# The routed-expert stage of a one-layer decoder kernel: expert block in another order, weight pieces of 1 MB, x gathered straight into its tile

## The reference

```python
e_flat = eidx.reshape(-1)                 # 1024 tokens x 8 experts
...
padded = (counts + EXPERT_BLOCK - 1) // EXPERT_BLOCK * EXPERT_BLOCK   # blocks of 128 rows, each of one expert
...
xb = x_pad[row_tok].reshape(n_blocks, EXPERT_BLOCK, d)

def expert_block(args):
    xblk, e = args
    hid = jax.nn.silu(xblk @ w_gate[e]) * (xblk @ w_up[e])
    return hid @ w_down[e]

yb = lax.map(expert_block, (xb, block_e)).reshape(n_rows, d)
y = jax.ops.segment_sum(yb * row_w[:, None], row_tok, num_segments=t + 1)
```

## Time and profile before

| | |
|---|---|
| median of 3 runs | 2982.41 us (2974.08 to 2987.12) |
| the profiled execution, its time | 2998.25 us |
| its span in the profile | 2996.7 us |
| PE busy over the span | 2573.5 us (86%) |
| expert stage, 1865 to 2850 us: PE busy | 901.49 of 985 us |
| the same stretch: DVE, ACT, POOL busy | 669.34, 602.02, 414.89 us |
| the same stretch: share of DMA time in use | 0.78 |

### The profile page before, as it was taken

The page is one execution under the profiler, slowest core; times in us unless marked ns, Lnnn a source line. Parts: engine busy times, 40 slices in busy tenths (PEclk is TensorE's granted clock), DMA queues, the critical chain, the costliest instruction groups (busy, mean ns, idle before and its releaser), DMA issues. The chain is left out here.

```text
span 2996.7 us, 39317 instructions
## 1 busy us (share of the span) xinstructions
PE 2573.5 (86%) x12548; PEld 2072.5 (69%) x12549; DVE 1864.5 (62%) x2441; ACT 1264.2 (42%) x1673; POOL 766.6 (26%) x888
## 2 busy tenths in 40 slices
PE   7989998998999999969977832899999989998956
PEld 5768777777877777747856721677777767776832
DVE  3346887787788655527446613676677676667428
ACT  3343453354345333335221102566566675566400
POOL 2012111222211111100002072444444444444300
PEclk9999999999999999989989965999999999999978
DMA  5423345342322353263543135788778787879367
GB/s 117 67 44 63 64 47 53 64 57 50 78 54 47 71 78 78 61 207 123 170 149 105 60 72 171 249 282 274 256 279 284 268 304 261 263 262 331 129 268 320
DMA packets 246349, 462.96 MB, mean 154 GB/s; under 512 B 26649, under 2 KB 151065, under 8 KB 244191
## 3 DMA queue, kind: packets, MB, share of 16 engines
q1 hardware_dynamic: 211870, 377.44, 45.1%
q0 software_dynamic: 34368, 84.04, 8.0%
HBM read 399.97 MB, written 93.87 MB: 165 GB/s over the span
## 5 line engine op out<-in xcount | busy, mean ns | idle before, releaser
L58 PE MATMUL dn_pj<-x_hi,dn_hi 128*128 128x512 f32 x1024 | 437.7, 427 | 5.1 <-DVE dn_lo L924 2.9
L60 PE MATMUL dn_pj<-x_hi,dn_lo 128*128 128x512 f32 x1024 | 411.0, 401 | 0.0
L59 PE MATMUL dn_pj<-x_lo,dn_hi 128*128 128x512 f32 x1024 | 409.8, 400 | 0.0
L1008 DVE SCALAR_TENSOR_TENSOR uc_half<-u_in,par,uc_half 128x512 f32<-128x512 f32 x480 | 383.3, 798 | 13.1
L2250 DVE TENSOR_TENSOR e_lo<-e_raw,e_hi 128x1024 fp32r<-128x1024 f32 x256 | 340.4, 1389 | 74.1 <-ACT e_hi L2193 68.0
L58 PE MATMUL gu_ps<-e_hi,xg_hi 128*128 128x512 f32 x744 | 317.8, 427 | 56.2 <-DVE xg_lo L2255 32.0
L2193 ACT ACTIVATE e_hi<-e_raw 128x1024 fp32r<-128x1024 f32 x256 | 251.9, 1052 | 141.6 <-DMA e_raw<-in_w_gate_e_dram 116.5
L60 PE MATMUL gu_ps<-e_hi,xg_lo 128*128 128x512 f32 x744 | 300.2, 403 | 0.0
L59 PE MATMUL gu_ps<-e_lo,xg_hi 128*128 128x512 f32 x744 | 300.0, 403 | 0.0
L1147 POOL TENSOR_TENSOR a_lvl<-a_t,lvl_mask 128x512 f32<-128x512 f32 x112 | 167.7, 1514 | 349.0 <-PE dn_a L686 221.1
L60 PEld LDWEIGHTS dn_pj<-x_hi,dn_lo 128*128 128x128 f32 x1024 | 198.5, 194 | 45.8
(11 more groups left out here) (346 smaller groups left out, 5183.1 us busy)
## 6 DMA issues: line engine op xcount, KB each, us to landing
e_raw<-in_w_gate_e_dram SPq DMA_DIRECT2D x128, 512.0 KB
e_raw<-in_w_up_e_dram SPq DMA_DIRECT2D x128, 512.0 KB
e_raw<-in_w_down_e_dram SPq DMA_DIRECT2D x128, 512.0 KB
dn_raw<-in_w_in_dram SPq DMA_DIRECT2D x64, 512.0 KB
y_rows<-y_rows SPq DMA_DIRECT2D x8, 2560.0 KB, 30.7
y_rows<-y_rows SPq DMA_DIRECT2D x8, 1536.0 KB, 25.1
gate_rows<-qkv_next SPq DMA_DIRECT2D x16, 512.0 KB, 3.1
br_raw<-in_w_oa_dram SPq DMA_DIRECT2D x16, 512.0 KB
```

What stands on the lines that cost most here:

```text
L58: nc.tensor.matmul(out, w_hi, x_hi, start=first, stop=False)
L59: nc.tensor.matmul(out, w_hi, x_lo, start=False, stop=False)
L60: return nc.tensor.matmul(out, w_lo, x_hi, start=False, stop=last)
L1008: ins = stt(out=uc[:], in0=u_in[:, t:t + HALF], scalar=w, in1=uc[:], op0=ALU.mult, op1=ALU.add)
```

## The change

The raw tiles become three of 1 MB, each filled by two DMAs of 512 KB: gate|up of k 0 to 3, gate|up of k 4 to 7, and down. ACT and DVE split each in one instruction. Gate|up is still split two experts ahead, down now one ahead, with semaphores of its own (`dhi_s`, `dlo_s`). On PE a block now is: wait for `hidden` of the block before, gate|up k 0 to 3, transposes of that `hidden`, transposes of the next x, the register loads for the next expert, gate|up k 4 to 7, down of the block before. ACT and DVE run the three splits between the other steps of a block. `x_landing` and POOL's copy are gone: the indirect DMA writes `x_gather` itself, and so is issued only when PE has transposed the block before. A second small DMA (`credit_d[1]`) sets `xg_in` off at 16.

```diff
-PIECES = 6
+GU = 2
 BUFS = 3
-SLOTS = 6
 LAG = 4
-raw = [sb(ctx, f"e_raw{q}", [P, 4 * FF]) for q in range(SLOTS)]
+raw = [sb(ctx, f"e_raw{i}", [P, 2, 4 * FF]) for i in range(GU + 1)]
...
-xl_d = sb(ctx, "x_landing", [P, D])
...
-    if i < 4:
-        ks, w = slice(4 * (i // 2), 4 * (i // 2) + 4), i % 2
-        return raw[i][:].rearrange("p (k f) -> p k f", k=4), wh[j][:, ks, w, :], wl[j][:, ks, w, :]
-    return raw[i][:], dh[j][:, i - 4, :], dl[j][:, i - 4, :]
+    if i < GU:
+        wkf = lambda w: w[j][:, 4 * i:4 * i + 4, :, :].rearrange("p k w f -> p w k f")
+        return raw[i][:].rearrange("p w (k f) -> p w k f", k=4), wkf(wh), wkf(wl)
+    return raw[i][:], dh[j][:], dl[j][:]
...
+    def load_gate_up(e, first):
+        for i in range(GU):
             if not first:
+                sp.wait_ge(lo_s, e * GU + (i + 1 - GU))
+            for n, w in enumerate((a["w_gate_e"], a["w_up_e"])):
+                src = w[0, bass.ds(e, 1)].rearrange("o (p k) f -> p (o k) f", k=KT)[:, 4 * i:4 * i + 4, :]
+                sp.dma_start(raw[i][:, n, :].rearrange("p (k f) -> p k f", k=4), src).then_inc(w_in[i], 16)
+    def load_down(e, first):
+        if not first:
+            sp.wait_ge(dlo_s, e)
+        for n in range(2):
+            src = a["w_down_e"][0, bass.ds(e, 1)].rearrange("o (c p) n -> p (o c) n", p=P)[:, n, :]
+            sp.dma_start(raw[GU][:, n, :], src).then_inc(w_in[GU], 16)
+    load_gate_up(0, True)
+    load_down(0, True)
+    load_gate_up(1, False)
+    with sp.Fori(2, E) as e:
+        load_gate_up(e, False)
+        load_down(e - 1, False)
+    load_down(E - 1, False)
...
-    def gather(n, column):
+    def rows(n, column):
         alone(pool, self.passed)
+        pool.wait_ge(xg_in, n * 16 + 16)
         g.tensor_copy(idx_g[:], self.tok_tab[:, column]).then_inc(idx_c, 1)
         g.tensor_copy(late_rows[:, bass.ds(n + LAG, 1)], self.row_tab[:, column]).then_inc(idx_l, 1)
         pool.wait_ge(idx_c, n + 1)
-        alone(pool, self.passed)
-        pool.indirect_dma_start(xl_d[:], None, self.x1_d, bass.IndirectOffsetOnAxis(idx_g[:, 0:1], 0),
-                                bounds_check=S - 1, oob_is_err=False).then_inc(xg_in, 16)
-    def hand_over(n):
-        pool.wait_ge(xg_in, n * 16 + 16)
+    def gather(n):
         pool.wait_ge(t_done, n * 2 + 2)
         alone(pool, self.passed)
-        g.tensor_copy(xg[:], xl_d[:]).then_inc(x_here, 1)
-        pool.wait_ge(x_here, n + 1)
+        pool.indirect_dma_start(xg[:], None, self.x1_d, bass.IndirectOffsetOnAxis(idx_g[:, 0:1], 0),
+                                bounds_check=S - 1, oob_is_err=False).then_inc(xg_in, 16)
     def scatter(n):
...
     with pool.Fori(0, E) as e:
-        nb, base = plan(pool, e)
+        nb, base = blocks(pool, e), first_block(pool, e)
         with pool.Fori(0, nb) as b:
             n = base + b
-            gather(n, bass.ds(e * NT + b, 1))
+            rows(n, bass.ds(e * NT + b, 1))
+            gather(n)
             scatter(n)
-            hand_over(n)
-    total = pool.value_load(self.plan[0:1, E - 1, 1:2], min_val=0, max_val=MAXB - 1) + \
-        pool.value_load(self.plan[0:1, E - 1, 0:1], min_val=1, max_val=NT)
+    total = first_block(pool, E - 1) + blocks(pool, E - 1)
     for late in range(LAG):
         scatter(total + late)
         if late == 0:
-            pool.wait_ge(t_done, total * 2 + 2)
-            pool.sem_inc(x_here, 1)
+            gather(total)
...
     def transposes(gb):
-        pe.wait_ge(x_here, gb + 1)
+        pe.wait_ge(xg_in, gb * 16 + 32)
         xv = xg[:].rearrange("p (c k) -> p k c", k=KT)
...
-    def down(j, gb):
+    def down(e, j, gb):
+        pe.wait_ge(dlo_s, e + 1)
         pe.wait_ge(hl_s, gb + 1)
...
-    def blk(e, j, j_prev, gb, first):
-        pe.wait_ge(xl_s, gb * 2 + 1)
-        if first:
-            pe.wait_ge(lo_s, e * PIECES + 2)
-        gate_up(j, range(0, 4))
-        pe.wait_ge(xl_s, gb * 2 + 2)
-        if first:
-            pe.wait_ge(lo_s, e * PIECES + 4)
-        gate_up(j, range(4, 6))
-        transposes(gb + 1)
-        gate_up(j, range(6, 8)).then_inc(gu_done, 1)
-        if j_prev is not None:
-            down(j_prev, gb - 1)
-        hid_t(gb)
...
+    def run(experts):
+        nb, base = blocks(pe, experts[0][0]), first_block(pe, experts[0][0])
+        for i, (e, j, _) in enumerate(experts):
+            following = experts[i + 1][0] if i + 1 < len(experts) else None
+            loaded = []
+            def blk(b, gb, first):
+                prev = not first or not isinstance(e, int) or e > 0
+                if prev:
+                    pe.wait_ge(hid_s, gb)
+                pe.wait_ge(xl_s, gb * 2 + 1)
+                if first:
+                    pe.wait_ge(lo_s, e * GU + 1)
+                gate_up(j, range(0, 4))
+                if prev:
+                    hid_t(gb - 1)
+                pe.wait_ge(xl_s, gb * 2 + 2)
+                transposes(gb + 1)
+                if first:
+                    if following is not None:
+                        loaded.extend((blocks(pe, following), first_block(pe, following)))
+                    pe.wait_ge(lo_s, e * GU + 2)
+                gate_up(j, range(4, 8)).then_inc(gu_done, 1)
+                if prev and first:
+                    down(e - 1, (j + BUFS - 1) % BUFS, gb - 1)
+                elif prev:
+                    down(e, j, gb - 1)
+            expert(pe, e, nb, base, blk)
+            if following is not None:
+                nb, base = loaded
     transposes(0)
-    all_experts(pe, expert)
-    nb, base = plan(pe, E - 1)
-    pe.wait_ge(lo_s, E * PIECES)
-    down((E - 1) % BUFS, base + nb - 1)
+    all_experts(pe, run)
+    nb, base = blocks(pe, E - 1), first_block(pe, E - 1)
+    pe.wait_ge(hid_s, base + nb)
+    hid_t(base + nb - 1)
+    down(E - 1, (E - 1) % BUFS, base + nb - 1)
...
-    def blk(gb, prev, split):
-        split(0, 1, 2, 3)
-        act.wait_ge(gu_done, gb + 1)
-        A(sg[:], gu[:, 0, :], ACT.Silu).then_inc(sg_s, 1)
-        for b in range(2):
-            act.wait_ge(t_done, gb * 2 + 5 + b)
-            x_hi(b)
-        if prev:
-            y_move(gb - 1)
-        act.wait_ge(ht_done, gb + 1)
-        A(hh[:], ht[:], ACT.Copy).then_inc(hh_s, 1)
-        split(4, 5)
...
+            def blk(b, gb, first):
+                def split(i):
+                    ahead = 2 if i < GU else 1
+                    if first and (not isinstance(e, int) or e + ahead < E):
+                        hi((j + ahead) % BUFS, nth + (j + ahead) // BUFS, i)
+                prev = not first or not isinstance(e, int) or e > 0
+                split(0)
+                if prev:
+                    hid_hi(gb - 1)
+                act.wait_ge(t_done, gb * 2 + 5)
+                x_hi(0)
+                split(1)
+                act.wait_ge(gu_done, gb + 1)
+                A(sg[:], gu[:, 0, :], ACT.Silu).then_inc(sg_s, 1)
+                act.wait_ge(t_done, gb * 2 + 6)
+                x_hi(1)
+                split(2)
+                if prev:
+                    y_move(gb - 1)
...
-    def blk(e, b, gb, split):
-        split(0, 1, 2, 3)
-        dve.wait_ge(sg_s, gb + 1)
-        v.scalar_tensor_tensor(out=hid[:], in0=sg[:], scalar=self.wt_tab[:, bass.ds(e * NT + b, 1)],
-                               in1=gu[:, 1, :], op0=ALU.mult, op1=ALU.mult).then_inc(hid_s, 1)
-        x_lo(gb + 1, 0)
-        x_lo(gb + 1, 1)
+    def hid_lo(gb):
         dve.wait_ge(hh_s, gb + 1)
         tt(hl[:], ht[:], hh[:].bitcast(F32), ALU.subtract).then_inc(hl_s, 1)
-        split(4, 5)
...
+                split(0)
+                if not first or not isinstance(e, int) or e > 0:
+                    hid_lo(gb - 1)
+                x_lo(gb + 1, 0)
+                dve.wait_ge(sg_s, gb + 1)
+                v.scalar_tensor_tensor(out=hid[:], in0=sg[:], scalar=self.wt_tab[:, bass.ds(e * NT + b, 1)],
+                                       in1=gu[:, 1, :], op0=ALU.mult, op1=ALU.mult).then_inc(hid_s, 1)
+                x_lo(gb + 1, 1)
+                split(1)
+                split(2)
```

127 lines of the change are left out of this document (58 added, 69 removed).

## The result

| | before | after |
|---|---|---|
| median | 2984.01 us (2974.08 to 2987.12, 4 runs) | 3110.49 us (3097.31 to 3114.42, 4 runs) |
| ratio, 95% interval | | 1.0422 [1.0381, 1.0463] |
| span of the profiled execution | 2996.7 us | 3112.9 us |

The account below looks back on a forecast made before the run. PE, busy 86% of the span, was taken as the bound, with the raw tile's loop longest in runs. Savings of 26 us outside runs and 20 in them, 46 from 2982.4, gave 2937 us; range 2887 to 2976.

Parts of the forecast that it names:

- The two regimes: Expert stage: later blocks bound by PE; runs of one-block experts with PE, DVE, ACT and DMA all heavily used.
- PE's floor: Expert stage: a block's 46 matmuls take PE at least 9.43 us at full clock.
- The waits for x's low part, for `hidden` and for registers: PE's waits of 32.0, 28.0 and 22.8 us: first mostly gone, second loses its place, about 15 of the third gone.
- Landing copy and sizes of the splits: DVE saves 0.68 us per first block without POOL's copy; doubled splits take at most 2.44 us on DVE, 2.10 on ACT.
- So it is hidden and costs nothing: The direct gather, issued about 4.1 us into a block, has 8.4 us to land and needs at most 7.1.
- The 4.7: Gather's landing time, 4.7 us from its issue to the start of its copy, in the profile before.
- is issued earlier relative to nothing: The scatter behind the gather must land before `y_block` is written, a wait of 32.2 us in 12 cases before.
- no change: Rival: y's late scatter holds ACT at `y_block`, 45 us go back in 64 first blocks, time 2982 us; chance 0.14.
- One of the prediction's own signs of being wrong: The forecast is wrong if ACT waits for the scatter in most blocks.
- slower: the raw tile's loop: Rival: a 1 MB tile refills only once wholly split; a 7.0 us load gives 13.2 us periods, 3010 us; chance 0.10.
- The landing of 4.9 us: Load of 1 MB into a raw tile, making the loop 11.1 us and saving 20 us in the runs.
- What was forecast for the new order: PE's waits for `hidden` and x's low part mostly go; the 57 periods outside runs fall to 9.6 us, saving 26.

Follow-up runs that it names:

- e8: The changed kernel with six pieces of 512 KB instead of the 1 MB pieces; 3020.4 us, ratio 1.0114 to the kernel before.
- e7: The kernel before with the new order alone, keeping 512 KB pieces and the landing copy; 3023.3 us, ratio 1.0135.
- e13: The changed kernel with POOL's steps reordered, scatter ahead of the wait for the landed gather and the next gather; 3033.1 us, ratio 1.0145.
- e10: The changed kernel with DVE's split of each 1 MB piece made in two halves; 3067.2 us, ratio 1.0274 to the kernel before.
- e12: The changed kernel with 512 KB pieces and POOL's steps reordered so the scatter precedes the gather's wait; 2964.3 us, ratio 0.9909.
- e18: e12 with ACT's `hid_hi` and DVE's `hid_lo` moved between the two 512 KB splits; 2960.6 us, ratio 0.9903 to the kernel before.

## Why the prediction was wrong

**What bounds the kernel.** The two regimes and PE's floor held: later blocks take 9.3 us wherever nothing stalls. The waits for x's low part, for `hidden` and for registers went about as counted (32.0 to 1.4, 28.0 to 12.0 in one wait, 22.8 to 7.9 us).

**Landing copy and sizes of the splits.** Right and small. DVE's split of 2048 took 2.29 us and ACT's 1.91, against bounds of 2.44 and 2.10. With direct gather a DVE split of 1024 takes 1.22 us in e8. But e7 and e8 differ by 3 us: without the copy and with the later gather the time is nearly the same.

**"So it is hidden and costs nothing": the gather.** It held for PE, which waited 11.2 us in the stage beyond the start, though the gather landed in 7.2 us, not 4.7. The 4.7 was the start of a copy, and 26 waits of the copy say when a gather was late, not how long it usually takes under another load.

**The scatter: the step that failed.** The forecast's own sum has no term for it: the scatter "is issued earlier relative to nothing" and stands at zero. It was counted only as a rival, "no change", with a sum of 4.1 + 1.0 + 1.1 + 4.7 = 10.9 against 9.4 for the end of down, 1.5 us late, of which 0.7 us would reach PE in each first block. All three terms were too small. From transposes to scatter it is 3.8 us, not 2.1: 0.9 us pass between the end of the transposes and the gather, which the sum left out, so that about 3.05 us is the least; and the row that gave 1.1 was taken where no DVE split lay beside the index copy, while the change made that split twice as long. Landing took 6.6 us, not 4.7; the way through DVE that the prediction named was given no size. And of the 238 us by which `y_block` was late, PE waited 153, or 2.4 us for each first block, since ACT's split, DVE's split and `hid_lo` stand in series behind `y_block`: ACT's 25 us free of 85 was cited against it, but free time counts only if it lies between `y_block` and `hid_hi`. The mechanism had the right place, and a third of its size. 0.14 went to it, with its end at 2982 us; no case held 3110. One of the prediction's own signs of being wrong came true: ACT waited for the scatter in 63 of 93 blocks.

**Larger pieces: the mis-sized landing.** The rival "slower: the raw tile's loop" put the decision where landing passes 6.2 us and named 13.2 us for 7.0. Measured in e13: 6.6 us and 12.18 for the loop shown. The landing of 4.9 us that the forecast's sum took was too short, and the rival had it nearly right; it was given 0.10, since the sum took "at most one other tile" to be in flight. Its period for the runs was too long, though: 11.44 us in the mean. In the changed kernel itself it hardly shows (ACT waits 19.7 us for weights), since the late scatter leaves the loads time; it shows when the scatter is cured. The splits' length also fed the scatter: e10's 44 us.

**Rivals as exclusive cases.** They were weighed one against another, and their prices lie on the same path in turn: change to e13 83 us for the scatter, e13 to e12 69 us for the pieces. Less the 27 us by which e12 is faster than the kernel before, that makes the 126 us up to one. What was forecast for the new order was right in direction, but only with POOL's steps rearranged and small pieces: e12 is 27 us and e18 31 us faster than before.

## What to carry to other kernels

- A transfer that is issued behind a new wait has to be followed to the next buffer it frees, and all that stands in series behind that buffer's writer is its price. Take its landing from the same kind of DMA under the load it will meet, and from the long end.
- Before pieces are made larger, write down the loop split, free, load, split for one tile. Larger pieces save instructions and take away early release, for the tile, for POOL beside DVE, and for small steps queued behind.
- If one gain hides behind two losses, undo each alone and both together: here the new order paid only once both were undone.
